# Attention on TensorE: a finished group's values products placed before the step's gate product

## The reference, cut to what matters

```python
s = einsum("q h d, k h d -> h q k", q, k) + bias      # scores
p = softmax(s)
o = einsum("h q k, k h d -> q h d", p, v)             # values
y = o * silu(gate)                                    # gate = x @ w_gate, a projection as large as the output
```

## Time and profile before

| | before |
|---|---|
| median of 3 runs | 2519.25 us |
| lowest and highest run | 2516.83 and 2521.42 us |
| span of the profiled execution, first to last instruction | 2514.3 us |
| PE busy | 2441.7 us (97%) |
| PEld busy | 1978.6 us (79%) |
| DVE busy | 1679.6 us (67%) |
| ACT busy | 1106.6 us (44%) |
| mean granted TensorE clock | 0.995 |

### The profile page before, as it was taken

The page is one execution under the profiler, slowest core; times in us unless marked ns, Lnnn a source line. Parts: engine busy times, 40 slices in busy tenths (PEclk is TensorE's granted clock), DMA queues, the critical chain, the costliest instruction groups (busy, mean ns, idle before and its releaser), DMA issues.

```text
span 2514.3 us, 37056 instructions
## 1 busy us (share of the span) xinstructions
PE 2441.7 (97%) x14414; PEld 1978.6 (79%) x14414; DVE 1679.6 (67%) x3270; ACT 1106.6 (44%) x2069; POOL 0.2 (0%) x4
## 2 busy tenths in 40 slices
PE   8999999999999999999999999999999999999998
PEld 6878898788888778798987888888866666788666
DVE  6777577464447885675865544488686676599775
ACT  4346355443223343454544333333456676232563
POOL 0000000000000000000000000000000000000000
PEclk9999999999999999999999999999999999999999
DMA  4320152223337432202412332573210001132311
GB/s 160 90 77 27 51 153 75 76 82 94 101 113 230 151 93 83 73 3 85 150 51 70 107 101 93 184 219 111 68 34 18 18 18 34 51 95 66 86 41 59
DMA packets 74093, 219.29 MB, mean 87 GB/s; under 512 B 21312, under 2 KB 21568, under 8 KB 73152
## 3 DMA queue, kind: packets, MB, share of 16 engines
q1 hardware_dynamic: 48384, 176.06, 22.7%
q10 hardware_dynamic: 25536, 40.87, 5.3%
HBM read 214.80 MB, written 2.10 MB: 86 GB/s over the span
## 4 chain that ended last, share of the span: by engine, by line
PE 85%; DVE 9%; ACT 3%; issue 2%; ACTq 0%; DMA 0%; DVEq 0%
PE bank L602 21%; PE bank L603 20%; PE bank L604 20%; PE bank L843 4%; PE bank L879 3%; PE bank L853 3%; DVE w_lo L564 2%; PE bank L633 1%; PE bank L635 1%; PE bank L634 1%; ACT w_hi L557 1%; PE bank L659 1%; PE bank L661 1%; PE bank L660 1%; DVE e_s L953 1%
## 5 line engine op out<-in xcount | busy, mean ns | idle before, releaser
L557 ACT ACTIVATE w_hi<-w_raw 128x1024 fp32r<-128x1024 f32 x334 | 353.7, 1060 | 554.2 <-PE bank L604 513.8
L564 DVE TENSOR_TENSOR w_lo<-w_raw,w_hi 128x1024 fp32r<-128x1024 f32 x334 | 407.8, 1223 | 224.9 <-ACT w_hi L557 223.8
L602 PE MATMUL bank<-a_hi,w_hi 128*128 128x512 f32 x1344 | 533.4, 397 | 20.0 <-DVE w_lo L564 18.2
L604 PE MATMUL bank<-a_hi,w_lo 128*128 128x512 f32 x1344 | 524.6, 390 | 0.0
L603 PE MATMUL bank<-a_lo,w_hi 128*128 128x512 f32 x1344 | 524.2, 390 | 0.0
L602 PEld LDWEIGHTS bank<-a_hi,w_hi 128*128 128x128 f32 x1344 | 251.4, 187 | 82.0 <-issue 18.2
L604 PEld LDWEIGHTS bank<-a_hi,w_lo 128*128 128x128 f32 x1344 | 251.1, 187 | 55.5
L603 PEld LDWEIGHTS bank<-a_lo,w_hi 128*128 128x128 f32 x1344 | 251.4, 187 | 51.4 <-issue 1.0
L602 PE MATMUL bank<-b_hi,w_hi 128*128 128x512 f32 x440 | 182.5, 415 | 4.0 <-DVE w_lo L564 2.6
L603 PE MATMUL bank<-b_lo,w_hi 128*128 128x512 f32 x440 | 172.8, 393 | 0.0
L604 PE MATMUL bank<-b_hi,w_lo 128*128 128x512 f32 x440 | 172.4, 392 | 0.0
(11 more groups left out here) (462 smaller groups left out, 4496.8 us busy)
## 6 DMA issues: line engine op xcount, KB each, us to landing
w_raw<-w_tiles SPq DMA_DIRECT2D x334, 512.0 KB, 3.6
mod_raw<-mod_tiles ACTq DMA_DIRECT2D x48, 512.0 KB, 4.2
d_bias<-rpb_rows ACTq DMA_DIRECT2D x16, 224.0 KB, 4.4
hT<-xT ACTq DMA_DIRECT2D x8, 256.0 KB, 6.1
m_in<-memT ACTq DMA_DIRECT2D x2, 1024.0 KB, 4.7
mod_cond<-cond_rows ACTq DMA_DIRECT2D x2, 1024.0 KB, 5.8
out<-hT ACTq DMA_DIRECT2D x8, 256.0 KB, 2.2
ctx_sq<-ctxT ACTq DMA_DIRECT2D x1, 1024.0 KB, 7.6
```

The costliest lines, as they stand in the source:

```text
L557: act.activation(w_hi[:, t % SPLIT, :], w_raw[:, t % RAW, :], ACT.Copy).then_inc(sem("w_rounded"), 1)
L564: dve.tensor_tensor(w_lo[:, t % SPLIT, :], w_raw[:, t % RAW, :], w_hi[:, t % SPLIT, :].bitcast(f32), ALU.subtract).then_inc(sem("w_split"), 1)
L602: pe.matmul(o, wh, chunk(hi, k, n), start=k == 0, stop=False)
L604: mm = pe.matmul(o, wl, chunk(hi, k, n), start=False, stop=k == kc - 1)
```

## The change

`attention_pe` gets an argument `values_first`. With it the values of a finished group are issued directly behind the scores of the step, before the blocks of the gate product; the transposes then follow the gate product. It is turned on in the four attentions named above, not in the cross attention. It holds only while there are scores to issue (`i < len(steps)`); in the last turns of the loop the order stays.

```diff
@@ attention_pe
-                         turn_first=0):
+                         turn_first=0, values_first=False):
...
                 if i < len(steps):
                     att_scores_pe(pe, key, steps[i], units)
+                if values_first and pending is not None and i < len(steps):
+                    att_values_pe(pe, key, units, group_of(units, pending), terms)
+                    pending = None
                 if fill:
                     for _ in range(blocks(i)):
                         next(fill, None)
@@ second_pe, even
-... e_s, [(pair_tiles(e_pt), even_values)], turn_first=2,
+... e_s, [(pair_tiles(e_pt), even_values)], turn_first=2, values_first=True,
@@ second_pe, odd
-                         fill=odd_gate_steps(pe), blocks=lambda i: 4, turn_first=1,
+                         fill=odd_gate_steps(pe), blocks=lambda i: 4, turn_first=1, values_first=True,
@@ tensor stream, ("att", l)
-                             fill=gate_steps(pe, l), blocks=...
+                             values_first=True, fill=gate_steps(pe, l), blocks=...
```

More of the change, by code:

```diff
@@ L2717, in second_pe @@
             even_in_pe(pe)
-            attention_pe(pe, ("even",), even_units(), e_s, [(pair_tiles(e_pt), even_values)], turn_first=2,
+            attention_pe(pe, ("even",), even_units(), e_s, [(pair_tiles(e_pt), even_values)], turn_first=2, values_first=True,
                          need=[("e_roped", f"aq{CC - 1}"), ("e_kd", 0, 1, 1), ("e_vt_in", "bv", 1)],
@@ L3262, in _ @@
                              need=[("roped", l, i) for i in range(4)] + [("avt_in", l, 1)],
-                             fill=gate_steps(pe, l), blocks=lambda i: (GATE_BLOCKS + [0])[min(i, len(GATE_BLOCKS))],
+                             values_first=True, fill=gate_steps(pe, l), blocks=lambda i: (GATE_BLOCKS + [0])[min(i, len(GATE_BLOCKS))],
                              last=(lambda: gdn_rows_pe(pe, l, 0), lambda: (gdn_rows_pe(pe, l, 1), gdn_grams_pe(pe, l, 0))))
```

## The result

The changed kernel takes 2560.91 us (median of 4 runs, 2558.53 to 2563.17); the kernel before on the same chip 2520.34 us. The ratio is 1.0159, with a 95% interval of 1.0144 to 1.0175: 40 us slower. The forecast was 2552, with 2536 to 2564 as its range.

What follows compares the result with a forecast made beforehand. PE was taken as the bound, its order mattering only through gaps. Waits 42.4 - 0.6 already there - 4.8 gain - 4 given back = +33.0 us, span 2514.3 to 2547.3, median 2552 us; range 2536 to 2564.

Steps and rivals of the forecast that it cites:

- What bounds it, and how often: PE, 85% of the chain and busy 97% of the span; 32 of 40 values products move.
- The gain of 4.8 us: On PE, one change of array form fewer in each of 32 steps, 0.15 us each; bounds 0 and 10 us.
- The waits: Moved values on PE wait for ACT's last copy of transposed tiles: 31 waits, 42.4 us, paid in full.
- What is given back: Later transposes and scores on PE wait less for DVE and ACT: 4 us, between 0 and 5.9.
- The clock: PE's granted clock may fall to 1.2 GHz after long waits, losing 1.7 us per fall.
- one or two falls at most: Clock falls on PE that the forecast left within its range, outside the 8% case of a result above it.
- The rival: PE's clock falls after new waits: +8 us, 2560, for five falls; +53 us, 2605, for all 31; 8%.
- the five waits of about 2 us or more: New waits of values in the first stack (2.6, 2.6 us) and odd attention (2.05, 2.05, 1.8 us).
- The 5.0 us: Median of the runs before, 2519.25 us, lies this far above the profiled span of 2514.3 us; added to the forecast span.
- The copies keep up: ACT and DVE finish the copies 0.4 to 2.4 us sooner, waits vanish, 4.8 us gain remains: 2514.5 us; 3%.
- Half is absorbed: Stages behind the values give back 30 us of waits, result within 5 us of before; 4%.

Runs made afterwards that it cites:

- the first stack alone: Against the kernel before, values moved ahead of the gate product only in the two first-stack layers; 2531.0 us, ratio 1.0044.
- the three profiles: Two profiles of the changed kernel (2560.91 us) and one of the kernel before with values first in the even attention only (2543.83 us).
- the paired copies: Changed kernel, with ACT copying both lanes' transposed tiles behind the first lane's exponential instead of each behind its own; 2521.63 us, ratio 1.0004.
- the same kernel idling: Against the kernel before, values first in the even attention only, with no zero multiplications in the waits; 2543.83 us, ratio 1.0096.

## Why the prediction was right, and what it missed

**What bounds it, and how often.** Right. The order on PE is all that changed. PE's busy time grew by 2.4 us and the span by 42.4: the difference is idle time of PE.

**The gain of 4.8 us.** Right in size: 0.15 us a step, scores to values like scores to gate. In the first stack alone the sum closes with it to 0.1 us. The Trainium skill (TensorEngine Tiling (Array Packing), section "Tiling Modes") says that a change of mode drains the array. The 0.15 us agree with it in sign.

**The waits.** Read off one timeline each, they came to 42.4 us less the 0.6 already there, 41.8; measured 41.2. By attention: even 26.8 and 26.7, odd 9.0 and 8.7, first stack 6.6 - 0.6 and 5.8. The time from ACT to PE was 0.25 us at each of the 34 waits. Single waits of the even attention were off by up to 0.2 us both ways (priced 0.78, 0.87, 1.44 and 1.22 us, measured 1.01, 0.80, 1.40 and 1.09; the third of the banded half, priced like the second at 1.22, was 1.37), so an agreement of the sum to 0.6 us is in part luck. That the chains on ACT and DVE start from rest each time, so that nothing is caught up, fits with waits of such sizes; no run tests it by itself.

**What is given back.** Taken as 4 us. Waits plus half of the low time added, minus growth: even 26.7 + 5.1 - 26.0 = 5.8, of which 22 x 0.15 = 3.3 are boundaries and 2.5 given back; odd 8.7 - 5.9 = 2.8 at equal low time, 0.9 and 1.9; first stack 0. Together 4.4 us. Right in size.

**The sum without the clock** is thus 41.2 - 4.8 - 4.4 = +32.0 us beside +33.0 forecast. The span grew by 42.4.

**The clock** is the term that was mis-sized. The prediction left "one or two falls at most" inside the range and put 0 into the sum. In the profile of the changed kernel the first stack grew by 5.4 + 4.2 us where waits and boundaries make 5.2, so 4.4 us are the clock's; in even it is 5.1 us; the rest of the program adds 0.9 us. That is the missing 10 us between the two profiles, and by the medians, 2560.91 beside 2520.34, it is 8.6 us. One of the prediction's own signs of being wrong, a clock below 0.99 in the even attention, came true: it was 0.98, 0.97 and 0.98 in the three profiles. The forecast stood in spite of that, as its range left 12 us above it for a term that measured some 9 to 10. The rival priced it at 8 us for falls after the five waits of about 2 us or more. The size is near. The place is right in part: in the first profile three of these five had falls, in the second none. In the even attention falls followed waits of 1.1 to 1.5 us, which I had taken as harmless. The Trainium skill (TensorE: Matmul & The Clock Gate, section "A second HAM failure mode: psum-queue depth-cycling") tells of small idles between groups of matmuls that make the clock swing. The rows of the even attention agree, with 0 us low without the waits and 10 to 17 with them. I named the rule and then gave its mechanism no term.

**From span to median.** The 5.0 us that I took as lying around the instructions are two things. Each time that is listed for a profiled execution is 1.8 us above its span (2558.53 and 2556.7, 2518.84 and 2517.0); by that the other 3.2 us are that the profiled execution of before was faster than the median. The forecast of a median is not harmed by it.

**The rivals.** "The copies keep up" needed them 0.4 to 2.4 us sooner; the paired copies give them that, and even then the waits for DVE, 11.4 us instead of 7.0, take the gain, so 2514 was not reached either (2521.63). "Half is absorbed": 4.4 of 41.2 us was. Its 2535 us was counted with the forecast, though it lay just outside the range.

## What to carry to other kernels

Before an instruction block is moved ahead, ask what ran under the block that it passes: here the gate product was worth 0.15 us as a neighbour and up to 2.6 us as a cover. The price can be read from the trace of before, as the end of the last operand, plus the hand-over time, minus the new place's start, if the chain that makes the operand starts from rest. Where PE is nearly always busy, add to new waits a share for falls of the clock, 1.7 us each here; behind the moved values of the even attention it came to a fifth to a quarter of the waits.

## What was not expected of the hardware

Falls of the clock followed waits of 1.1 to 1.5 us that stood some 10 us apart with PE busy in between: 3 or 4 in 275 us in three profiles, none in nine profiles of the same attention without the waits. With multiplications by zeros in part of these waits the clock stayed up there, and the stretch was 5.4 us shorter than in the same kernel idling. The medians, 2539.97 and 2543.83 us, go the same way, but the ratios against before, 1.0077 and 1.0096, have intervals that overlap.
